# Where the last projection products, a gate wait and three output products stand at the end of an attention layer

## The reference, cut to what matters

```python
proj = h @ w_in                                   # h: RMSNorm(x), 1024 columns
q, k, v, qm, z = split(proj)                      # 3 groups x 4 heads of 128; z: the gates
for g, (win, dil) in enumerate(DIL_GROUPS):       # (128,1), (512,4), (2048,16)
    o, l = dilated_group_prompt(q[:, :, g], k[:, :, g], v[:, :, g], dil, win, bias_g)
alpha = softmax(stack(lses), axis=0)              # groups combined by their denominators
o = einsum('gbth,gbthe->bthe', alpha, stack(outs))
om = mem_attend(qm, mem_k, mem_v)                 # 256 memory tokens
return (concat([o, om]) * silu(z)) @ w_out, new_bufs
```

## Time and profile before

| | us |
|---|---|
| median of 3 runs (lowest, highest) | 2191.96 (2190.51, 2194.2) |
| the profiled execution: its own time | 2194.7 |
| the profiled execution: span | 2192.7 |
| PE busy | 2154.7, 98% |
| mean granted clock of PE | 0.997 of full |

### The profile page before, as it was taken

How to read it: one execution, slowest core, us unless ns; L and a number is a source line. 1 busy time by engine, 2 the same in 40 slices (tenths; PEclk the granted TensorE clock), 3 DMA queues, 4 the chain that set the end, 5 groups by cost and what they waited for, 6 DMA issues and landing times.

```text
span 2192.7 us, 46735 instructions
## 1 busy us (share of the span) xinstructions
PE 2154.7 (98%) x19630; PEld 1531.5 (70%) x19630; DVE 938.3 (43%) x2431; ACT 663.8 (30%) x1589; POOL 456.4 (21%) x642
## 2 busy tenths in 40 slices
PE   8999999999999999999999999999999999999998
PEld 6888888888888876544567667676676666665444
DVE  5234354354344444321355555555555233333252
ACT  4122321312222131311234434444344344442101
POOL 0522241242123205000032322322322110020000
PEclk9999999999999999999999999999999999999999
DMA  7412211212221166666012212122110173114451
GB/s 227 154 42 64 81 30 41 78 43 67 58 59 42 35 212 227 213 207 212 13 62 93 70 74 83 67 79 80 60 53 14 40 273 97 39 59 148 136 168 53
DMA packets 210278, 210.99 MB, mean 96 GB/s; under 512 B 14262, under 2 KB 181654, under 8 KB 209151
## 3 DMA queue, kind: packets, MB, share of 16 engines
q1 hardware_dynamic: 198070, 148.27, 22.4%
q0 software_dynamic: 12000, 59.73, 7.1%
HBM read 179.56 MB, written 68.23 MB: 113 GB/s over the span
## 4 chain that ended last, share of the span: by engine, by line
PE 50%; DVE 0%; ACT 0%; issue 0%; POOL 0%; DVEq 0%
PE bank L2088 19%; PE bank L2802 8%; PE bank L3292 7%; PE bank L2146 4%; PE bank L2162 4%; PE bank L2144 2%; PE bank L2154 1%; PE bank L2818 1%; PE bank L2827 1%; PE bank L3270 1%; PE bank L3303 0%; PE bank L2177 0%; PE bank L3199 0%; PE bank L3176 0%; PE bank L2810 0%; PE bank L3186 0%
## 5 line engine op out<-in xcount | busy, mean ns | idle before, releaser
L884 PE MATMUL bank<-arena 128*128 128x256 f32 (+1 forms) x2688 | 631.7, 386 | 0.0
L884 PEld LDWEIGHTS bank<-arena 128*128 128x128 f32 x2688 | 494.5, 190 | 75.3
L2088 PE MATMUL bank<-arena 128*128 128x352 f32 x1296 | 469.2, 474 | 0.1
L2088 PEld LDWEIGHTS bank<-arena 128*128 128x128 f32 x1296 | 214.0, 190 | 58.1 <-ACT arena L2309 0.6
L2802 PE MATMUL bank<-arena 128*128 128x352 f32 x576 | 176.4, 459 | 0.0
L3292 PE MATMUL bank<-arena 128*128 128x512 f32 x360 | 167.5, 599 | 0.0
L2146 PEld LDWEIGHTS bank<-arena 128*128 128x128 f32 x864 | 125.5, 192 | 36.7 <-issue 0.3
L2802 PEld LDWEIGHTS bank<-arena 128*128 128x128 f32 x576 | 106.6, 190 | 53.3
L2162 PEld LDWEIGHTS bank<-arena 32*32 32x32 f32 x7680 | 78.8, 105 | 91.6 <-issue 39.8
L1338 POOL TENSOR_TENSOR arena<-arena 128x272 f32<-128x272 f32 (+1 forms) x48 | 31.5, 656 | 507.6 <-ACT arena L1058 487.6
L2146 PE MATMUL bank<-arena 128*128 128x128 f32 x864 | 131.3, 278 | 0.2 <-ACT arena L2329 0.2
(11 more groups left out here) (426 smaller groups left out, 2720.2 us busy)
## 6 DMA issues: line engine op xcount, KB each, us to landing
arena<-in_w_in_a SPq DMA_DIRECT2D x48, 512.0 KB, 5.1
arena<-in_w_in_b SPq DMA_DIRECT2D x40, 512.0 KB, 4.1
arena<-in_cache_win_k SPq DMA_DIRECT2D x48, 256.0 KB, 5.1
arena<-in_cache_win_v SPq DMA_DIRECT2D x48, 256.0 KB, 3.6
out<-arena SPq DMA_DIRECT2D x40, 256.0 KB, 3.3
arena<-in_w_mem_kv SPq DMA_DIRECT2D x16, 512.0 KB, 8.0
arena<-in_cache_mem_k SPq DMA_DIRECT2D x32, 256.0 KB, 4.1
arena<-in_cache_mem_v SPq DMA_DIRECT2D x32, 256.0 KB, 3.4
```

The costliest lines, as they stand in the source:

```text
L884: m = nc.tensor.matmul(o[:, 0:hi - lo], w, y, start=k == 0 and i in (0, 1, 3, 5), stop=k == KH - 1, skip_group_check=i in (2, 4, 6))
L2088: m = nc.tensor.matmul(bank[j % 3][:, 0:PART], ring.slots[:, (B1 + b) % RING, k, :], part_in(k, part_), start=k == 0, stop=k == KD - 1)
```

## The change

Five edits, all in layer A. `needs` asks for two tasks less ahead of a memory stage. `segments` takes six products of the last but one stage away from its units and gives them to its tail, and splits the rest over eight units in place of seven. PE runs three of the four first output units earlier: unit 0 ahead of the last `mem_turn`, unit 1 behind it, unit 2 behind the last values; unit 3 stays behind the fourth turning. VectorE waits for the gates' Silus ahead of the first output of a memory stage (in unit 1) and not at the stage's start.

```diff
--- before.py
+++ after.py
@@ -713,7 +713,7 @@
     NTASK = 2 * NPAIR
     FIRST_TASKS = 4
     TURNS = (6, 6, 8, 0)
-    needs = lambda s: {0: 12 * (s // 4) + 4, 1: 12 * (s // 4) + 6, 2: 12 * (s // 4) + 10, 3: 12 * (s // 4) + 12}[s % 4]
+    needs = lambda s: {0: 12 * (s // 4) + 4, 1: 12 * (s // 4) + 6, 2: 12 * (s // 4) + 10, 3: 12 * (s // 4) + 10}[s % 4]
 
     def segments():
 
@@ -721,15 +721,16 @@
         for s in range(NSTAGE):
             g = s % 4
             end = min((FIRST_TASKS + 3 * (s + 1)) * PER_TASK, NTASK * PER_TASK)
-            more = s + 2 < NSTAGE
+            more, late = s + 2 < NSTAGE, s + 2 == NSTAGE
+            end -= 6 * late
             for n in range(TURNS[g]):
                 out[(s, "turn", n)] = at_, at_ + int(n >= 2 and at_ < end)
                 at_ = out[(s, "turn", n)][1]
-            first, over = at_, 8 if more else 7
+            first, over = at_, 8 if more or late else 7
             for u in range(8):
                 out[(s, "u", u)] = at_, first + (end - first) * min(u + 1, over) // over
                 at_ = out[(s, "u", u)][1]
-            out[(s, "tail", 0)] = at_, at_ + ((6 if g == 3 else 10) if more else 0)
+            out[(s, "tail", 0)] = at_, at_ + ((6 if g == 3 else 10) if more else 6 * late)
             at_ = out[(s, "tail", 0)][1]
             for n in range(4 if g == 3 else 0):
                 out[(s, "last", n)] = at_, at_ + int(more)
@@ -1029,15 +1030,19 @@
             turn_probs(s, 7)
             beside(s, "tail", 0)
             if s == NSTAGE - 1:
+                first_out_unit(0)
                 mem_turn(7)
+                first_out_unit(1)
             values(s, 7)
+            if s == NSTAGE - 1:
+                first_out_unit(2)
             if g == 3:
                 pe.wait_ge(comb_o, h + 1)
                 for t in range(4):
                     turn(EBASE[3] + 56 * h + 8 + t, [(c, ocomb[:, 2 * t + c, :]) for c in range(2)])
                     if s + 2 < NSTAGE:
                         beside(s, "last", t)
-                    else:
+                    elif t == 3:
                         first_out_unit(t)
 
     @block.scalar
@@ -1238,8 +1243,6 @@
         for s in range(NSTAGE):
             h, g = s // 4, s % 4
             e = EBASE[g] + 56 * h
-            if g == 3:
-                dve.wait_ge(z_silu, 2 * (h + 1))
             if g < 3:
 
                 after(dve, kv_out, 16 * (8 * h + (0, 2, 4)[g]))
@@ -1271,6 +1274,8 @@
                 normed(s, u)
                 for ev in ended((s, "u", u), True):
                     evacuate(*ev)
+                if u == 1 and g == 3:
+                    dve.wait_ge(z_silu, 2 * (h + 1))
                 if u:
                     outputs(s, u - 1)
                 if u and s == NSTAGE - 1:
```

## The result

The changed kernel takes 2199.24 us in the median of 22 runs (2193.18 to 2205.35), the kernel before 2192.77 in 22 runs of the same series (2189.18 to 2198.19). The ratio is 1.0030, 95% interval 1.0023 to 1.0038: **slower by about 6.5 us**, beyond the 0.2% that I called the bound, and above my range (2189.2 to 2195.0). The profiled execution took 2196.89 us, span 2194.8.

The account below looks back on a forecast made before the run. TensorE, busy 98% of the span, was taken as the bound, leaving only idle or low-clock time to gain. Stage 14 and border +0.1, output units -0.1: 0.0 us, applied to the 2191.96 median, forecast 2192.0, range 2189.2 to 2195.0.

Parts of the forecast that it names:

- Units 0 to 2: Stage 14: the gate wait loses its cover; unit 2's turning restarts at 782.39, idle there growing from 1.37 to about 3.6 us.
- The clock there: Behind stage 14's new hole: one 3.4 us stretch at half clock, costing +1.5 us, with 0 and 3.4 as ends.
- case A: The forecast: gate wait uncovered, one half-clock stretch follows, border cured; within 1 us of before; chance 0.50.
- case C: Like the forecast, but the low clock lasts twice as long, as at the border; +1.7 us, 2193.7; chance 0.12.
- the row of the 1.37 us hole: Stage 14, before unit 2's turning: this hole did not lower the clock; by it alone the sum would be -1.4.
- The border: Between stages 14 and 15: idle falls from 3.46 to 0.5 us; 1.41 us earlier if the clock never falls.
- my sum: Stage 14 and the border together: -1.4 from the border, +1.5 from the clock, making +0.1 us.
- Needs and gate wait: Memory stage of each head: fewer tasks awaited by PE, VectorE's wait for the Silus moved; nothing waits, 0.
- Output units: End of stage 15: moved output units fill a hole, turnings lose cover; PE's next phase 0.1 us earlier, -0.1.
- Rival D: Stage 14's gate wait doesn't grow and the border's 6 us go, with 0.5 left; -5.5 us, 2186.5; chance 0.06.
- step on the transposed memory: Border: its load lands at 799.51, 0.3 us before the first memory block needs it; SyncE's later loads cost nothing.
- rival E: Border: the transposed memory's load lands late; slower beyond the bound, over 9.5 us of landing needed to pass +4.4; chance 0.04.

Follow-up runs that it names:

- segments alone: The kernel before with only the six products kept for stage 14's tail and the even split of the other 34: 2197.18 us, +3.1 against before.
- block loads first: The changed kernel, with SyncE issuing memory block 4's load before waiting for the partials' store and blocks 5 to 7 before the cache tiles: 2199.78 us, +5.2 against before.
- filled kernels: Unread matmuls put into PE's idle holes: at the border in the kernel before, 2196.36 us; at the gate in the changed kernel, 2201.35 us.

## Why the prediction was wrong, step by step

**Right.** *Units 0 to 2.* The turning of unit 0 came with 0.65 us of idle (forecast 0.19 + 0.46), unit 0's values with 0.73 of idle from the copy that I had named, unit 2's turning at 780.24. All of this kernel's early times lie 2.26 us below those of before, so my 782.39 becomes 780.13. *The clock there.* It fell for one short stretch, case A, in the first profile and the third; for 6.8 us, case C, in the second. The Trainium skill's rule, that the burst behind such a wait starts cold ("TensorE: Matmul & The Clock Gate", section on HAM oscillation), is borne out: all five traces with these two holes (three of the changed kernel, segments alone, block loads first) show it, and the row of the 1.37 us hole would have misled. *The border.* 0.66 us of idle, forecast 0.5, released by VectorE's add. The kept memory landed in time. At 803 us the three profiles are 0.6, 1.9 and 0.7 us behind, my sum was +0.1, so this term was short by 0.5 to 1.8 us; the 1.8 is case C. *Needs and gate wait*: 0, measured +0.8 with 0 well inside the interval. *Output units*: -0.1 forecast, -0.05 between 836 and 846 us in the trace, and no difference when alone. *Rival D's side* was rightly judged unlikely: the gate wait did grow.

**Wrong, first.** The step on the transposed memory says that SyncE's later loads "go out some 12 us before the third memory block or the weights need them, and cost nothing". I followed blocks 2 and 3, and not blocks 4 to 7, which stand on the same queue behind the partials' round trip. Block 4 cost 1.55, 1.3 and 2.58 us of wait, and in the third profile a further fall of the clock. Between 803 and 830 us, where block 4 stands, the three profiles lost 1.8, 1.6 and 4.5 us. My rival E named a late load, but the wrong one, and it held that nothing shares the queues then, where two weight blocks went out 2.5 us behind the kept memory's load (it still landed in 4.8 us, forecast 4.6). That taking the loads out of the queue changes the local time is shown (the wait goes, 1.7 us and more in stages 14 and 15); it pays in the median only together with the covered gate (-2.3 to -4.6).

**Wrong, second.** The sum stopped at stage 15: I took the rest of the kernel as shifted, not changed, and gave the half-clock stretches and the idle holes elsewhere no term and no width. The three profiles of the changed kernel took 1336.1, 1337.0 and 1335.6 us for it, against 1334.1 before. In place of 0.0 the three executions came to 2.4, 3.4 and 5.2 us in the edited stages and 2.0, 2.9 and 1.5 behind them, together 4.4, 6.4 and 6.7, about the measured +5.0 to +6.5. The edited stages have the larger part in each.

What the rest's time consists of is read from the traces: for the changed kernel it is more half-clock time (10.2 to 13.7 us against 6.8) at about the same or less idle time (12.4 to 14.5 against 14.1), for the filled kernels more idle time. What **remains open** is why PE's instructions come late at other places from one kernel to the next, and from one execution to the next: the changed kernel's first profile has the holes near 1340, 1347 and 1540 us, its second near 1306 and 1386. My attempt to predict the rest from the shift failed, and one profile for each kernel can't give a distribution.

The gate's cover is the part of the cause that the runs do settle: the same 34 products, split so that five stand behind the gate again and units 3 to 7 get fewer, turn +5 to +6.5 into -2.3.

## What to carry to other kernels

When work is moved to fill a hole, look for the hole that it filled until now: six products cured a border of 3.46 us of idle and uncovered a gate five units earlier. When PE gains time, follow every load on the queue to its next user, the ones far behind too, for the slow place may have been their cover. And where a kernel's runs spread with the mean clock, a few us of expected gain or loss need a term for the half-clock stretches elsewhere, or a range that holds them. Where PE's idle time is put down to "issue", look at the DMA records of the queue "instruction" ahead of it, before a theory of the clock is built on it.

## What was not expected of the hardware

Filling PE's idle time with useless matmuls kept the granted clock at 1.00 through the border (six matmuls, 1.3 us gained in place), and the kernel was 2.1 us slower in the whole. PE stood idle for up to 2.44 us with no semaphore to wait for, each time until 1.21 to 1.64 us after a 16 KB packet of instructions had landed. A 512 KB load took 8.3 to 9.5 us to land while cache tiles and output weights were under way around it, at 347 to 404 GB/s, against 4.2 and 5.4 us for two of the same size in the kernel before when only the kept memory was under way beside them; so a load's lead must be reckoned at the queue's load. And the same changed kernel took 2195.46 to 2204.46 us in twelve runs on one chip; its three profiles differ in nothing larger than the number and place of their half-clock stretches, the place of the idle holes ahead of these, and the length of block 4's wait.
